# Tile 1's gate projections beside the expert gathers, down rows requested four turns ahead, routing at turns 1, 3, 5 and 8

## The reference, cut to what matters

```python
proj = h @ w_in[layer]                       # ... gate_sb, gate_d are its last 2 x 1024 columns
merged = jax.nn.sigmoid(gate_sb) * br_sb + jax.nn.sigmoid(gate_d) * br_d
x = x + gt1[:, None, :] * (merged @ w_out[layer])
h2 = modulate(rms_norm(x, g_ffn[layer]), sh2, sc2)
q = (h2 @ w_pq).reshape(T, 8, 2, 128)        # 8 heads, two halves
sub = einsum('thpc,hpnc->thpn', q, peer_keys)
s_top, i_top = top_k(sub, 16)                # per half; then the best 16 of 16 x 16 pairs
expert = take_along_axis(cand_i, pos)        # 16 of 16384 experts per token and head
u = peer_u[expert]; act = gelu(einsum('cd,ckd->ck', h2, u))
v = peer_v[expert]; out = einsum('ck,ckd->cd', gate * act, v)
```

## Time and profile before

| what | value |
|---|---|
| time, median of 3 runs | 1525.46 us (1525.05 to 1528.88) |
| time of the profiled execution | 1530.73 us |
| its span | 1528.9 us |
| busy: PE, DVE, POOL, ACT | 87%, 47%, 37%, 20% of the span |
| mean granted clock of PE | 0.945 of full speed |
| read from HBM | 505.35 MB, 331 GB/s over the span |
| gathers: two groups of 256 | 274.5 and 289.3 us of POOL |

### The profile page before, as it was taken

One profiled execution on the slowest core, in us unless ns is written; L12 is line 12 of the kernel. 1 busy time (PEld: TensorE's weight loads), 2 busy tenths in 40 slices (PEclk: granted clock), 3 DMA queues, 4 the chain that ended last, 5 costly groups with the idle time before them and its releaser, 6 DMA issues.

```text
span 1528.9 us, 13787 instructions
## 1 busy us (share of the span) xinstructions
PE 1325.2 (87%) x4656; PEld 753.3 (49%) x4656; DVE 724.1 (47%) x1642; ACT 304.1 (20%) x735; POOL 570.9 (37%) x531
## 2 busy tenths in 40 slices
PE   6999999567897896895798999899888998999997
PEld 6868689433454563443344455343333344554443
DVE  5125242585764666565765676655535322220001
ACT  1131111331221112221231321111110122411102
POOL 1000000366777667776764556546554100000000
PEclk8899999788998999998899999999999999999999
DMA  9845544589999999999999999999999889688882
GB/s 395 325 172 184 221 164 164 175 302 370 353 354 389 405 408 404 409 398 364 376 410 410 408 409 409 409 409 409 409 410 408 295 306 411 221 253 276 287 301 91
DMA packets 135284, 507.33 MB, mean 332 GB/s; under 512 B 15408, under 2 KB 16304, under 8 KB 133168
## 3 DMA queue, kind: packets, MB, share of 16 engines
q0 software_dynamic: 75456, 293.63, 49.2%
q1 hardware_dynamic: 58320, 208.63, 37.4%
q10 hardware_dynamic: 1440, 4.19, 0.8%
HBM read 505.35 MB, written 1.05 MB: 331 GB/s over the span
## 4 chain that ended last, share of the span: by engine, by line
PE 49%; DMA 21%; another core or an unknown queue 9%; DVE 8%; issue 5%; POOL 4%; ACT 3%; SPq 0%; DVEq 0%; ACTq 0%; POOLq 0%
PE ps_M L843 18%; DMA arena<-in_peer_u,arena 14%; PE ps_M L398 7%; PE ps_T L644 6%; PE ps_T L645 5%; DMA ring<-in_w_second 3%; DMA ring<-in_peer_v,arena 3%; DVE tmp L1877 3%; POOL ring L1111 2%; PE ps_M L408 2%; PE ps_M L590 2%; PE ps_S L419 2%; PE ps_M L619 2%; POOL arena L1098 1%
## 5 line engine op out<-in xcount | busy, mean ns | idle before, releaser
L843 PE MATMUL ps_M<-ring,arena 128*128 128x512 f32 x1088 | 497.5, 600 | 12.5 <-DMA ring<-in_w_second 8.8
L1098 POOL DMA_INDIRECT arena<-in_peer_u,arena x256 | 274.5, 1072 | 252.0 <-DVE tmp L1877 100.0
L1111 POOL DMA_INDIRECT ring<-in_peer_v,arena x256 | 289.3, 1130 | 172.0 <-issue 64.6
L644 PE MATMUL ps_T<-ring,arena 128*128 128x512 f32 x436 | 240.5, 635 | 106.0 <-ACT arena L1249 54.7
L843 PEld LDWEIGHTS ps_M<-ring,arena 128*128 128x128 f32 x1088 | 203.2, 192 | 251.3 <-issue 241.4
L645 PE MATMUL ps_T<-ring,arena 128*128 128x512 f32 x436 | 233.4, 618 | 0.0
L1877 DVE SCALAR_TENSOR_TENSOR tmp<-arena,merged 128x1024 f32<-128x1024 f32 x128 | 156.8, 1225 | 143.2 <-DMA arena<-in_peer_u,arena 127.1
L1877 DVE SCALAR_TENSOR_TENSOR tmp<-arena 128x1024 f32<-128x1024 f32 x128 | 156.3, 1221 | 66.9 <-DMA arena<-in_peer_u,arena 51.2
L644 PEld LDWEIGHTS ps_T<-ring,arena 128*128 128x128 f32 x436 | 77.5, 199 | 201.3 <-issue 140.3
L645 PEld LDWEIGHTS ps_T<-ring,arena 128*128 128x128 f32 x436 | 86.9, 199 | 111.9 <-issue 111.9
L398 PE MATMUL ps_M<-hT,ring 128*128 128x256 f32 x576 | 129.9, 385 | 1.3 <-ACT hT L1262 1.3
(11 more groups left out here) (257 smaller groups left out, 1092.7 us busy)
## 6 DMA issues: line engine op xcount, KB each, us to landing
ring<-in_w_second SPq DMA_DIRECT2D x276, 512.0 KB, 4.6
arena<-in_w_ada POOLq DMA_DIRECT2D x12, 2048.0 KB, 10.8
ring<-in_w_in SPq DMA_DIRECT2D x46, 512.0 KB, 8.3
ring<-in_w_pq SPq DMA_DIRECT2D x32, 512.0 KB
ring<-in_w_out SPq DMA_DIRECT2D x16, 512.0 KB, 4.0
ring<-in_w_br SPq DMA_DIRECT2D x16, 384.0 KB, 3.1
arena<-in_peer_u,arena POOLq DMA_INDIRECT x256
ring<-in_peer_v,arena POOLq DMA_INDIRECT x256
```

Source lines behind the costliest of these rows:

```text
L644: low = mm(twin[:, 0:512], dg[:, i % 8, :], v_ring[n % VR][:, 0:512], start=first, stop=last)
L843: m = mm(bank, left[c], w[:, c, :], start=first and c == 0, stop=last and c == 1)
L1098: pool.indirect_dma_start(u_ring[:, n % UR, :], None, A["peer_u"][0], bass.IndirectOffsetOnAxis(ap=expert[:, u % 3, k:k + 1], axis=0))\
L1111: pool.indirect_dma_start(v_ring[n % VR], None, A["peer_v"][0], bass.IndirectOffsetOnAxis(ap=expert[:, u % 3, k:k + 1], axis=0))\
```

## The change

The sixteen gate tiles are used twice: `tile_gate(0, ...)` makes tile 0's gates in stage one, with 128 columns a matmul, and `tile_gate(1, ...)` tile 1's in phases -1 to 2, four tiles a phase at turns 1, 4, 9 and 12, from tiles that SP loads again under the names "lga" and "lgb". ACT's tanh of them is split the same way (`gate_tile`, turns 2, 5, 10, 13). POOL requests the down row of turn k + 4 (`AHEAD`) together with the up row of turn k, and waits for the list of experts only ahead of the up gather. DVE's routing moves to turns 1, 3, 5 and 8. For the first unit, the norm's sum is taken in eight parts between the matmuls of `out1`, the scores are made and copied by halves, and routing waits for a half at a time. `stick_scores1(0)`, its copy (`stick_old(0)`) and its mask (`stick_mask1(0)`) go behind the first unit's scores and routing.

```diff
+def late_gates(phase):
+    return [(("lga", "lgb")[n % 2], n // 2) for n in range(4 * (phase + 1), 4 * (phase + 2))]
...
+    elif phase < 3:
+        FIRST += late_gates(phase)[:2] + [(f"q{u}", 0), (f"q{u}", 1)] + late_gates(phase)[2:]
...
+            def tile_gate(t, name):
+
+                bank = claim_m(name)
+                w = tile(name)
+                for c in range(KC):
+                    m = mm(bank[:, 0:P], w[:, c, :], hT[:, c, tile_tok(t)], start=c == 0, stop=c == KC - 1)
+                finish(m, name)
...
+            def norm_part(c):
+
+                pe.wait_ge(sq_ready, KC + c + 1)
+                m = mm(ps["SA"][:, 0:P], ones[:, :], squares[:, c, :], start=c == 0, stop=c == KC - 1)
...
+            def half_scores(half):
+
+                name = ("sub", 0, half)
+                bank = claim(("OT", "T0")[half], name)
+                pe.wait_ge(*emptied(("q0", half)))
+                finish(mm(bank[:, 0:NK], qT[:, half, :], keysT[:, half, :], start=True, stop=True), name)
...
-                both_tiles(("ga", c))
-                both_tiles(("gb", c))
+                tile_gate(0, ("ga", c))
+                tile_gate(0, ("gb", c))
...
-            stick_scores1(0)
             for k in range(KC):
                 out1(0, k)
-            tile_norm("SA", ("norm2", 0), 1)
+                if k == 1:
+                    claim("SA", ("norm2", 0))
+                if k > 0:
+                    norm_part(k - 1)
+            norm_part(KC - 1)
...
+                if phase < 3 and k in (1, 4, 9, 12):
+                    tile_gate(1, late_gates(phase)[(1, 4, 9, 12).index(k)])
...
             for phase in range(-1, NU):
-                if phase + 1 < NU:
-                    pool.wait_ge(idx_ready, phase + 2)
                 for k in range(TOPK):
-                    if phase >= 0:
-                        gather_v(phase, k)
+                    if k < TOPK - AHEAD and phase >= 0:
+                        gather_v(phase, k + AHEAD)
+                    elif k >= TOPK - AHEAD and phase + 1 < NU:
+                        gather_v(phase + 1, k + AHEAD - TOPK)
                     if phase + 1 < NU:
+                        if k == 0:
+                            pool.wait_ge(idx_ready, phase + 2)
                         gather_u(phase + 1, k)
...
-            stick_mask1(0)
             own()
             for k in range(KC):
                 out1_update(0, k)
...
             route_index(0)
+            stick_mask1(0)
...
-                    if k in (2, 5):
-                        route_half(u, (k - 2) // 3)
+                    if k in (1, 3):
+                        route_half(u, k // 3)
+                    elif k == 5:
+                        route_best(u)
                     elif k == 8:
-                        route_best(u)
-                    elif k == 11:
                         route_index(u)
```

More of the change, by code:

```diff
@@ L36 @@
 UR, VR = 6, 8
+AHEAD = 4
 ARENA = 28964
@@ L599, in tile_norm @@
                 finish(m, name)
+            def norm_part(c):
+                pe.wait_ge(sq_ready, KC + c + 1)
+                m = mm(ps["SA"][:, 0:P], ones[:, :], squares[:, c, :], start=c == 0, stop=c == KC - 1)
+                if c == KC - 1:
+                    finish(m, ("norm2", 0))
             def turn_rows(t, half, b):
@@ L755, in _ @@
                 query(0, half)
-            scores(0)
+                half_scores(half)
             for half in range(2):
                 turn_rows(0, half, f"T{half}")
+            stick_scores1(0)
             for half in range(2):
@@ L1022, in source @@
                     return w_in_v[:, 24 + n, :]
-                if what in ("ga", "gb"):
-                    return w_in_v[:, 30 + KC * ("ga", "gb").index(what) + n, :]
+                if what[-2:] in ("ga", "gb"):
+                    return w_in_v[:, 30 + KC * ("ga", "gb").index(what[-2:]) + n, :]
                 if what in ("br0", "br1"):
@@ L1249, in diagonal, with gate_tile @@
                 F(dg[:, i % 8, :], ident[:, :], ACT.Copy, scale=wgt[:, u % 2, k:k + 1]).then_inc(diag_ready, 1)
+            def gate_tile(t, s, c, name):
+                act.wait_ge(*produced(name))
+                F(gate[:, t * KC + c, s, :], ps[use[name][0]][:, 0:P], ACT.Tanh, scale=0.5).then_inc(released(name), 1)
             act.wait_ge(vec_in, 16)
@@ L1303, in _ @@
                 for s, name in enumerate((("ga", c), ("gb", c))):
-                    act.wait_ge(*produced(name))
-                    F(gate[:, c:c + KC + 1:KC, s, :], ps[use[name][0]][:, 0:T].rearrange("p (t n) -> p t n", n=P),
-                      ACT.Tanh, scale=0.5).then_inc(released(name), 1)
+                    gate_tile(0, s, c, name)
                 if c == 1:
@@ L1316, in _ @@
                     dil_take(0, 1)
-            stick_old(0)
             F(warm[:, 1:2], eps, ACT.Sqrt)
@@ L1325, in _ @@
                 query_take(0, half)
-            score_take(0)
+                copy(("sub", 0, half), sub[:, 0, half, :], NK)
             for half in range(2):
                 copy(("rows", 0, half), h_rows[0][:, half * 512:(half + 1) * 512], 512)
+            stick_old(0)
             for half in range(2):
@@ L1396, in beside @@
                     copy(("gt2", k - 9), gt2_row[:, (k - 9) * 512:(k - 8) * 512], 512)
+                if phase < 3 and k in (2, 5, 10, 13):
+                    name = late_gates(phase)[(2, 5, 10, 13).index(k)]
+                    gate_tile(1, ("lga", "lgb").index(name[0]), name[1], name)
                 if phase + 3 < NU:
@@ L1783, in merge @@
                     dve.wait_ge(merged_tile, KC * t + c - 1)
+                dve.wait_ge(*emptied((("gb", "lgb")[t], c)))
                 dve.wait_ge(*produced((f"br{t}", c)))
@@ L1826, in route_half @@
             def route_half(u, half):
-                if half == 0:
+                if u == 0:
+                    dve.wait_ge(*emptied(("sub", 0, half)))
+                elif half == 0:
                     dve.wait_ge(*emptied(("sub", u)))
```

## The result

The changed kernel took 1550.95 us (median of 4 runs, 1537.71 to 1558.01), the kernel before 1526.93 (4 runs, 1525.05 to 1528.88). The ratio is 1.0127, 95% interval 1.0084 to 1.0169. The forecast was 1509 us with a range of 1498 to 1521: wrong in sign, and outside the range. The profiled execution of the change took 1545.63 us (span 1543.8) against 1530.73 (1528.9) before: the medians stand 24.0 us apart, the two profiled executions 14.9, so what follows accounts for the smaller of the two.

A forecast was written before the change was run, and what follows sets the result against it. Bounds: PE in stage one, a PE-DVE-ACT chain to the first gather, transfers at 409 GB/s from 770 to 1195 us. -23 - 2 + 9 + 0 = -16 from 1530.73 gives 1514.7; median 5.3 lower: 1509 us, range 1498 to 1521.

The forecast's parts named there:

- Term 1: Stage one: tile 0's gates at 128 columns a matmul, with one PE wait of some 4 us; -23 us, bounds -27 and -20.
- Term 2: Chain from merge to first gather: scores moved behind, norm in parts, scores by halves; -2 us, bounds -3.5 and -0.5.
- Term 3: Gather stage, phases 0 to 2: late gates and 8.39 MB loaded again, partly absorbed; +9 us, bounds -1 and +20.5.
- What would show it: Signs, including first gather at 262 to 267 us and phases 0 to 2 in 150 to 158 us at about 385 GB/s.
- Term 4: Gather stage: down rows four turns ahead and earlier routing exchange POOL's waits for like ones; 0 us, bounds -5 and +8.
- D: Rival, chance 0.09: POOL's stall at each unit's ninth down row runs transfers dry; 1554 us at 3 us a phase.
- B: Rival, chance 0.22: the gather stage absorbs all added bytes; Term 3 and Term 4 come to -4 to +3; 1500 us.
- C: Rival, chance 0.19: phases 0 to 2 stay at 365 GB/s by PE's order; late gates cost 20.5 us; 1515 to 1521.
- A: The forecast itself, chance 0.50: in the gather stage Term 3 and Term 4 together cost +4 to +14; 1504 to 1514 us.

The follow-up runs named there:

- group 1: Runs on one chip: the change with AHEAD = 0, 1504.92 us (0.9961); the same with both tiles' gates made before the gathers, 1510.46 us (0.9992).
- the pair: The change unaltered and its twin, differing only in AHEAD = 0, on one chip: 1544.59 and 1502.89 us, ratios to the kernel before 1.0215 and 0.9947.
- group 4: Runs on one chip: the kernel before, 1509.33 us in its profiled execution, and the change with AHEAD = 0, median 1502.47 us, ratio 0.9942.
- groups 1 and 5: Two sets of runs on the same chip; the kernel before took 1511.55 and 1510.47 us, and with only AHEAD = 4 added 1546.17 us (1.0221).

## Why the prediction was wrong

**Term 1 (-23): right.** The gates of tile 0 end at 216.40, 23.9 us earlier, with the one wait of 4.20 us ahead of the sum of chunk 9, forecast as 4. Of the 23.9, 2.8 were there when the gates began (175.02 against 177.79 in the earlier trace rows), so the gates themselves gave 21.1, inside the bounds. The same 2 to 3 us lie between other profiles of kernels whose stage one is the same up to there, so that part is no work of the change.

**Term 2 (-2): right.** From the end of the gates to the first gather it took 46.3 us instead of 49.2, -2.9. The first gather came at 262.70 (forecast 264.5).

**Term 3 (+9): inside its bounds, but set too low.** 188.4 - 178.2 = +10.2 us on one chip, by phases -1 to 2 of the change with AHEAD = 0 and of the kernel before; these two differ in more than the late gates. The two runs of group 1 with AHEAD = 0, with and without late gates, differ by +16.2 over the gather stage, nearer to the 20.5 of their bytes than to 9. One premise was weaker than the rows had said: of the room that the earlier trace rows show in phases 0 to 2, more than half was gone on the faster chips. Without late gates these phases run at

```profile
325.40:459.00 133.60, 118.38 (x424) 62.05 (x424) 95.70 (x244) 31.99 (x91) 104.32 (x97) 0.99 1.01 397
```

and with them they take 146.7 us at 408 GB/s. So PE's waits of the earlier trace rows did not decide; the transfers were full.

In the first comparison phases 0 to 2 of the change took 155.6 us at 380 GB/s, as "What would show it" had said (150 to 158 at about 385). That was luck: part of it is the loss by term 4.

**Term 4 (0): the step that failed.** It said that "a wait is exchanged for one of like size", and that "It costs nothing as long as what was requested before still runs: 8 gathers of 0.52 MB are 10.3 us of transfers". It measured +44.2 us in the pair (+41.7 in the medians), where the upper bound was +8. The earlier routing, counted in the same term, is worth nothing: 0.9950 with it at its old turns. Three things in it were wrong.

*The wait was priced at one place.* I priced the ninth down row alone, at 7 us a unit. But with eight slots and four turns ahead, every down row waits for the row eight before it, which PE adds four turns behind POOL. POOL waited for PE 108 times, 198.8 us in all. Added up over the trace, the ninth rows of the units have 69 us of that in fifteen waits, 4.6 each, less than the 7 that I gave them; the other 129 us, and 48.2 us of waits for DVE's adding, had no price in the sum.

*The stall was set too short where it was longest.* Weights plus 2 us for ACT and PE was the estimate; from unit 8's weights to the gather it was 735.44 - 723.75 = 11.7 us. In the pair, phase 8 lost 12.9 of the 44.2 us.

*What was in flight did not last.* In the stall of unit 8 POOL had issued its last gather by 725.72. The transfers went on at 406 to 422 GB/s up to 729, and then:

```profile
729.00:730.00 1.00, 0.00 (x0) 0.00 (x0) 1.00 (x2) 0.98 (x2) 0.00 (x0) 0.50 0.88 344
730.00:732.00 2.00, 0.59 (x1) 0.50 (x2) 1.96 (x5) 1.74 (x6) 0.00 (x0) 0.50 0.21 80
```

So what had been requested lasted some 4 us, not 10.3, against a stall of 9.71. POOL had come there with a gather every 1.24 us (0.94 and 0.30), while one takes 1.28 us of transfers at 409 GB/s: the eight gathers before the stall were not eight gathers in flight. With AHEAD = 0 more lies between issue and landing, 17 us in place of 9.2 by the median of the pair. In sum: length times (1 - GB/s / 409), added up over the phases, is 52 us of idle transfers in the change of the pair and 11 in its twin, which is nearly all of the 44.2.

**The rivals.** D, with a chance of 0.09, is what happened: the transfers run dry, and 44.2 us over 15 phases are 2.9 a phase. Its place was too narrow: the ninth rows have a third of POOL's waits for PE. That 3 us a phase gave 1554 and 1550.95 was measured is in part luck, since the same kernel stands 24 us above the kernel before in the first comparison and 34 on the chip of the pair. B and C were about the late gates and fell with A, since all three took term 4 as small; of the three, C had their price best (20.5 against 16.2 measured), but not its reason, since phases 0 to 2 did not stay at 365 GB/s. The sum for a version without AHEAD, -16, would have been nearer, but not right: on the faster chips it is -7 to -10 us (0.9942 to 0.9961). In the two profiles of group 4 the first gather of the kernel before is at 285.5 instead of 289.5, so the start gives 20 and not 25; +10.2 follow, and the tail is 4.1 longer (358.3 against 354.2): -5.7 us. These are single executions: on the chip of groups 1 and 5, the kernel before with AHEAD = 4 had its first gather at 289.5 again. In the first comparison only 41.0 us of 44.2 + 10.2 show, since the kernel before took 14.0 us longer in the gather stage there (881.8 us against 867.8): its idle transfers, by the sum above, are 40 us there and 23 in the profile of group 4.

The version that beats both kernels is the change with AHEAD = 0, 0.9942 to 0.9961 of the kernel before in four groups.

## What to carry to other kernels

A queue that requests two kinds of data in turn stops at whichever kind has no free slot, and the other kind stands behind it. A request moved n turns ahead, with the slots unchanged, takes n turns from the distance that the queue may run ahead of the consumer. Before moving a prefetch forward, compute slots minus turns ahead for each stream. Here 8 - 2 = 6, as much as the up rows have, cost next to nothing, and 8 - 4 cost 2.8%. The sum is a warning and not a price: 4 - 0 is the same 4 as 8 - 4 and cost half as much. And weigh a stall against what is in flight at that moment, by the time from issue to landing and by how long the transfers run on, not against the bytes of the last requests: eight gathers were 10.3 us of bytes, and lasted 4.

## What was not expected

The DMA share stays at 0.99 to 1.01 in stretches with 380 to 398 GB/s, and is 1.02 to 1.03 at 402 to 409. The share hides the loss; the GB/s shows it.

The kernel before takes 1510 to 1512 us on three chips (groups 1 and 5 ran on the same one), 1527 on that of the first comparison and 1536 on another, and its profile on a faster chip differs most in phases 0 to 2 (387 against some 365 GB/s). Why is not known.

PE's granted clock fell where PE waited: it was 0.50, the 1.2 GHz level, in the ten us from 723, in which PE was busy for 1.59, and its first two rows there took 2.05 and 1.92 us, where those from 736.22 on took 1.02. The mean over the span is 0.928 in the change of the pair and 0.957 in its twin.
